# The second product of an MLP as seven half-block products a step

## The chip, the cores and the metric

The kernel runs on one core of one Trainium2 chip. The metric is the device time of one execution in microseconds (us), here the median of three runs. Engines are named as in the profile: PE is TensorE, DVE is VectorE, ACT is ScalarE, POOL is GpSimd, SP is SyncE, which here only starts transfers. SBUF is the memory that all engines work in; PSUM holds the eight banks of 128 x 512 float32 into which PE writes.

## The reference, cut to what matters

One encoder layer over 1024 tokens of width 1024 in float32: a layer norm, an input projection, two kinds of attention, their merge, an output projection with a layer norm, and an MLP with a layer norm. The change is in the MLP alone:

```
h = layer_norm(DEEPNORM_ALPHA * h + merged @ w_out[l], ln1_g[l], ln1_b[l])
u = jnp.square(jax.nn.relu(h @ w_ff1[l]))             # (1024, 4096)
h = layer_norm(DEEPNORM_ALPHA * h + u @ w_ff2[l], ln2_g[l], ln2_b[l])
```

## The kernel before, in words

**Matmuls in three parts.** Every float32 operand of a matmul is kept as a high part (a copy rounded to PE's format) and a low part (value less high part). `three` (L500) multiplies high by high, high by low and low by high into one bank: three matmuls of 128 x 128 by 128 x 512 for each product of tiles. ACT makes high parts by a copy, POOL low parts by a subtraction.

**The MLP in 16 steps.** A step takes 256 of the 4096 hidden channels, as two tiles n = 0, 1. On PE, `hidden(s, n, half)` (L722) makes one tile of the hidden layer for one half (512) of the tokens: 8 x 3 matmuls into one of the two GEMM banks. Four such pieces are a step's first product. `result(s, slot)` (L731) makes the second product of a step: 16 banks (8 tiles of tokens by 2 halves of the output's columns), each 2 x 3 matmuls, over a ring of four banks. `pe_step` (L753) runs the hidden pieces of step s and then the results of the step before, so u and w_ff2 have two slots each and the splits of a step lie beside 43 us of PE's work.

**DVE.** `square` (L1477) takes a piece from its bank with relu and squares it in place in SBUF. `dve_step` (L1488) does four squares and then adds the 16 banks of the step before to `res`, the running sums (L1498; L1496 in the first step, with the residual's factor).

**ACT and POOL.** `act_step` (L1024) and `pool_step` (L1143) split, a step: two tiles of w_ff1 (128 x 1024 each; L1030, L1148), two tiles of w_ff2 at once (128 x 2048; L1034, L1151) and four pieces of u (128 x 512; L1038, L1155).

**SP.** `load_step` (L466) asks for one tile of w_ff1 when the last one's low part is done (two transfers of 256 KB), and for w_ff2's two rows of tiles (1 MB).

**The order** is written out by hand: each engine runs its own list, in loops over pairs of steps, and the lists meet in semaphores: `gemm_done`, `freed_dve` (bank read by relu), `u_full_done`, `u_hi`, `u_lo`, `w2_loaded`, `w2_hi`, `w2_lo`, `w_hi_done`, `w_lo_done`, `ring_done` (a bank of results is finished), `ring_read` (DVE has added it). In a loop the number waited for is computed from the step's number.

**The end.** After the last step DVE adds the last 16 banks with their row sums (L1515), ACT centres and squares (`centre_last`, L820), POOL multiplies with the gain (`gain`, L1064), DVE norms (`norm`, L1227) and SP stores, tile by tile.

## Time and profile before

| | |
|---|---|
| median of 3 runs | 1890.22 us (1889.5 to 1893.3) |
| the profiled execution's own time | 1891.27 us |
| span of its profile | 1889.5 us |
| PE busy | 1827.4 us, 97% of the span |
| DVE, ACT, POOL busy | 879.2, 615.2, 592.6 us |
| mean granted clock of PE | 0.992 of full speed |

The page of a profile gives the busy time of each engine over the span, then the same in 40 slices, then groups of instructions by line of the kernel. A table by stretches gives it for any part. In the order of time each row is an instruction, or some merged, with its start, its duration and in brackets how long the engine stood before it and who ended that. Matmuls overlap, so their pace is read from their starts, not from their durations (0.39 us).

### The profile page before, as it was taken

Reading aid. Unit: us, or ns where it says so; the run is one execution under the profiler, and the core shown is the slowest. Engines: PE = TensorE matmul, PEld = TensorE weight load, DVE = VectorE, ACT = ScalarE, POOL = GpSimd, SP = SyncE. Lnnn points to the kernel's source line nnn. Section 1 sums busy time; section 2 is a strip of 40 time slices with the busy share of each in tenths; the row PEclk is TensorE's granted clock in tenths of the full one; section 3 lists DMA queues with packets and bytes.
Section 4 is the critical chain, followed back from the end, with each engine's and each line's share of the span. In section 5 each row is a group of like instructions: output and inputs, shape, how many; then the busy total and the mean of one; then the engine's idle time right before and its main releaser. Section 6 shows DMA issues by size and latency. Waiting matters only on the chain.

```text
span 1889.5 us, 24837 instructions
## 1 busy us (share of the span) xinstructions
PE 1827.4 (97%) x9175; PEld 1489.9 (79%) x9175; DVE 879.2 (47%) x2053; ACT 615.2 (33%) x1339; POOL 592.6 (31%) x562
## 2 busy tenths in 40 slices
PE   6999999999999999999999899999999999999996
PEld 4777777777778888888888678888888888888884
DVE  6366666665665552013423466333333333333337
ACT  5355554555556664201222301211111111111104
POOL 4312111121134443222222480633333333333324
PEclk9999999999999999999999999999999999999998
DMA  7311111111111111144222510311111111111102
GB/s 249 116 36 45 33 47 34 34 46 33 42 40 32 36 30 34 45 134 144 79 79 90 194 40 23 123 45 45 44 44 44 44 44 54 63 49 55 33 0 89
DMA packets 143142, 117.91 MB, mean 62 GB/s; under 512 B 23300, under 2 KB 129996, under 8 KB 143052
## 3 DMA queue, kind: packets, MB, share of 16 engines
q1 hardware_dynamic: 133836, 112.52, 18.9%
q10 hardware_dynamic: 9216, 4.20, 0.8%
q8 instruction: 55, 0.90, 0.2%
q14 instruction: 35, 0.29, 0.1%
HBM read 99.88 MB, written 21.53 MB: 64 GB/s over the span
## 4 chain that ended last, share of the span: by engine, by line
PE 84%; DVE 7%; issue 3%; ACT 3%; POOL 2%; DMA 0%; POOLq 0%; SPq 0%; DVEq 0%; ACTq 0%
PE bank L502 25%; PE bank L504 24%; PE bank L503 24%; PE bank L538 4%; PE bank L526 3%; PE bank L586 2%; DVE mix L1321 2%; ACT mix L886 1%; PE bank L587 1%; DVE mix L1300 1%; DVE res L1236 1%; DVE o_buf L1288 1%; POOL hT_lo L1081 1%; DVE y_hi L1184 0%; POOL y_lo L1137 0%
## 5 line engine op out<-in xcount | busy, mean ns | idle before, releaser
L502 PE MATMUL bank<-hT_hi,w_hi 128*128 128x512 f32 x1312 | 528.8, 403 | 9.1 <-POOL hT_lo L1081 5.4
L503 PE MATMUL bank<-hT_lo,w_hi 128*128 128x512 f32 x1312 | 513.4, 391 | 0.0
L504 PE MATMUL bank<-hT_hi,w_lo 128*128 128x512 f32 x1312 | 513.3, 391 | 0.0
L1060 POOL TENSOR_TENSOR w_lo<-w_raw,w_hi 128x256 fp32r<-128x256 f32 x264 | 196.4, 775 | 630.6 <-ACT w_hi L777 630.6
L502 PEld LDWEIGHTS bank<-hT_hi,w_hi 128*128 128x128 f32 x1312 | 247.3, 188 | 82.5 <-issue 14.1
L504 PEld LDWEIGHTS bank<-hT_hi,w_lo 128*128 128x128 f32 x1312 | 247.4, 189 | 53.9
L503 PEld LDWEIGHTS bank<-hT_lo,w_hi 128*128 128x128 f32 x1312 | 247.8, 189 | 46.5
L502 PE MATMUL bank<-y_hi 128*128 128x512 f32 (+1 forms) x604 | 228.6, 379 | 2.7 <-DVE small L1515 2.7
L503 PE MATMUL bank<-y_lo,y_hi 128*128 128x512 f32 (+1 forms) x604 | 225.8, 374 | 0.0
L504 PE MATMUL bank<-y_hi,y_lo 128*128 128x512 f32 (+1 forms) x604 | 225.5, 373 | 0.0
L1498 DVE TENSOR_TENSOR res<-res,bank 128x512 f32<-128x512 f32 x224 | 154.1, 688 | 141.2 <-PE bank L504 141.2
L1484 DVE TENSOR_SCALAR mix<-bank 128x512 f32<-128x512 f32 x64 | 44.3, 691 | 255.9 <-PE bank L504 255.9
L1151 POOL TENSOR_TENSOR y_lo<-mix,y_hi 128x2048 fp32r<-128x2048 f32 x16 | 73.7, 4606 | 254.4 <-ACT y_hi L1034 254.4
L1155 POOL TENSOR_TENSOR y_lo<-mix,y_hi 128x512 fp32r<-128x512 f32 x64 | 83.6, 1308 | 166.3 <-ACT y_hi L1038 166.3
L1038 ACT ACTIVATE y_hi<-mix 128x512 fp32r<-128x512 f32 x64 | 40.4, 632 | 283.6 <-DVE mix L1486 283.6
L502 PEld LDWEIGHTS bank<-y_hi 128*128 128x128 f32 x604 | 113.8, 188 | 23.9 <-DVE small L1515 3.8
L504 PEld LDWEIGHTS bank<-y_hi,y_lo 128*128 128x128 f32 x604 | 113.9, 189 | 20.2
L503 PEld LDWEIGHTS bank<-y_lo,y_hi 128*128 128x128 f32 x604 | 114.0, 189 | 20.0
L1321 DVE CUSTOM_DVE_ANT_0 mix<-bank,aux 128x512 f32<-128x512 f32 (+2 forms) x192 | 99.0, 553 | 64.9 <-PE bank L538 64.5
L1034 ACT ACTIVATE y_hi<-mix 128x2048 fp32r<-128x2048 f32 x16 | 30.7, 1917 | 266.7 <-PE bank L504 263.1
L886 ACT ACTIVATE mix<-mix,small 128x256 f32<-128x256 f32 (+7 forms) x128 | 98.3, 770 | 42.8 <-DVE small L1329 42.3
L504 PE MATMUL bank<-y_hi,w_lo 128*128 128x512 f32 x256 | 99.6, 389 | 0.0
(154 smaller groups left out, 2674.5 us busy)
## 6 DMA issues: line engine op xcount, KB each, us to landing
w_raw<-in_w_in_dram SPq DMA_DIRECT2D x100, 256.0 KB, 3.3
w_raw<-in_w_ff_dram SPq DMA_DIRECT2D x64, 256.0 KB, 3.0
mix<-in_w_ff_dram SPq DMA_DIRECT2D x16, 1024.0 KB, 7.1
bias_rows<-bias_line SPq DMA_DIRECT2D x3, 1536.0 KB
res<-in_x_dram SPq DMA_DIRECT2D x8, 512.0 KB, 7.1
x_spill<-res SPq DMA_DIRECT2D x8, 512.0 KB, 5.9
o_spill<-o_buf ACTq DMA_DIRECT2D x64, 64.0 KB, 1.6
w_raw<-in_w_branch_b_dram SPq DMA_DIRECT2D x16, 256.0 KB, 3.9
```

The source lines that it names most:

```text
L502: pe.matmul(bank, lhs[0], rhs[0], start=start, stop=False)
L503: pe.matmul(bank, lhs[0], rhs[1], start=False, stop=False)
L504: return pe.matmul(bank, lhs[1], rhs[0], start=False, stop=stop)
L526: mm = pe.transpose(TR[n % 2][:, at * P:(at + 1) * P], src, ident[:, :])
L538: mm = pe.matmul(SC[units[m] % 3][:, at:at + keys.stop - keys.start], queries[left][rows], k[right][rows, k_slot, keys], start=not (left o ...
L886: e = act.activation(s_a[:, i % 2, m, 0:(i + 1) * P], s_a[:, i % 2, m, 0:(i + 1) * P], ACT.Exp, bias=neg_max[:, i % 2, m:m + 1], accum_out ...
L1060: ins = pool.tensor_tensor(w[1][:, n % 2, at:at + 2], w_raw[:, at:at + 2, :], w[0][:, n % 2, at:at + 2].bitcast(F32), ALU.subtract)
L1151: pool.tensor_tensor(w2[1][:, slot], w2_raw, w2[0][:, slot].bitcast(F32), ALU.subtract).then_inc(w2_lo, 1)
L1155: pool.tensor_tensor(u[1][:, slot, n, cols], u_full[:, n, cols], u[0][:, slot, n, cols].bitcast(F32), ALU.subtract).then_inc(u_lo, 1)
L1321: dve.tensor_tensor_reduce(out=s_a[:, slot, m, lo:hi], in0=SC[n % 3][:, 0:hi - lo], in1=bias_a[:, h % 2, off + lo:off + hi], scale=1.0, sc ...
L1484: dve.tensor_scalar(u_full[:, n, cols], GEMM[half][:, :], 0.0, None, ALU.max).then_inc(freed_dve, 1)
L1498: ins = dve.tensor_tensor(res[:, t, cols], res[:, t, cols], RING[g % 4][:, :], ALU.add)
```

## The change

In steps 0 to 14 the second product is computed by Strassen's scheme in its form with seven products and shared sums. The matrices of a step are cut in two each way: u (256 hidden channels by 1024 tokens) into four blocks of 128 x 512, w_ff2's two rows of tiles into four blocks of 128 x 512. DVE forms four differences of w_ff2's blocks and four sums or differences of u's blocks (`form`); with three raw blocks of each side (one of them replaced in place) that makes seven left and seven right factors. Each of the seven products is 4 banks (128 tokens each) of 3 matmuls, 28 banks a step, over a ring of six banks: the two banks that transposes used join the ring. Each product has its own running sum over all 15 steps (`sums_of`: four in `res`, two in `mix`, one in the last rows of y's two halves), and the sums are folded into the output once, beside the last step's hidden pieces. The residual is prepared for this in step 0 (two subtractions on `res`). The last step is computed as before, with tokens 512 to 1023 first.

u and w_ff2 now have seven slots of 128 x 512, and one set of them: full values lie where their low parts will be, and the splits are done in place. `result(s)` follows the hidden pieces of the same step s, so there is no lag of a step any more; the loops run over single steps. The hidden pieces come in the order (0,0), (0,1), (1,1), (1,0) of tile and half of tokens. w_ff2 comes in two transfers of 512 KB a step, the upper row once two products of the step before are done, the lower once all are. ACT and POOL split 14 blocks of 128 x 512 a step and two tiles of w_ff1.

The diff, cut to its core. Lines that are only deleted stand in the functions above.

```diff
+FF_ORDER = [(0, 0), (0, 1), (1, 1), (1, 0)]
+U_SLOT = [0, 2, 3, 5]
+PRODUCTS, QUARTER = 7, 4
+PER_STEP = PRODUCTS * QUARTER
+RING0 = 2 * NT
+TAIL0 = RING0 + PER_STEP * (FF_STEPS - 1)
+TAIL = [4, 5, 6, 7, 0, 1, 2, 3]
+TAIL_W2 = [0, 1, 5, 6]
...
-        u = [t[:, 0:4, :].rearrange("p (s n) q -> p s n q", n=2) for t in y]
-        w2 = [t[:, 4:8, :].rearrange("p (s n) c -> p s n c", n=2) for t in y]
-        w2_raw = mix[:, 0:2, :]
-        u_full = mix[:, 2:4, :]
+        y_full = [nc.alloc_sbuf_tensor_at(f"y_full{i}", [P, KT, SEQ], F32, offset=y_at + i * KT * SEQ * 4) for i in range(2)]
+        (u, w2), (u_full, w2_full) = (
+            [[t[:, :, :].rearrange("p s k -> p (s k)")[:, at:at + PRODUCTS * HALF].rearrange("p (s q) -> p s q", s=PRODUCTS) for t in pair]
+             for at in (0, PRODUCTS * HALF)] for pair in (y, y_full))
+        u_full, w2_full = u_full[1], w2_full[1]
+        first_sum = [t[:, 7, :].rearrange("p (t c) -> p t c", t=2) for t in y_full]
+        sums_of = [[first_sum[t // 2][:, t % 2, :] for t in range(QUARTER)],
+                   [mix[:, 2 + t // 2, t % 2 * HALF:(t % 2 + 1) * HALF] for t in range(QUARTER)],
+                   [res[:, 4 + t, HALF:DM] for t in range(QUARTER)],
+                   [res[:, 4 + t, 0:HALF] for t in range(QUARTER)],
+                   [mix[:, t // 2, t % 2 * HALF:(t % 2 + 1) * HALF] for t in range(QUARTER)],
+                   [res[:, t, 0:HALF] for t in range(QUARTER)],
+                   [res[:, t, HALF:DM] for t in range(QUARTER)]]
...
+        RING6 = RING + [banks[5], banks[6]]
...
+            def load_w2(s, row):
+                if row == 0:
+                    sp.wait_ge(ring_done, s * PER_STEP + (RING0 - PER_STEP + 2 * QUARTER) if not isinstance(s, int) or s else RING0)
+                else:
+                    sp.wait_ge(ring_done, s * PER_STEP + RING0)
+                at = s * 2 + row
+                src = ff2[:, bass.ds(at if isinstance(s, int) else sp.snap(at), 1), :]
+                sp.dma_start(w2_full[:, 5 * row:5 * row + 2, :], src.rearrange("p n (h c) -> p (n h) c", h=2)).then_inc(w2_loaded[row], 16)
+            def load_ff1(s, n):
+                sp.wait_ge(w_lo_done, s * 2 + (FF0 + n))
+                col = s * (2 * P) + n * P
+                col = col if isinstance(s, int) else sp.snap(col)
+                for g in range(2):
+                    sp.dma_start(w_raw[:, g * 4:g * 4 + 4, :], ff1[:, g * 4:g * 4 + 4, bass.ds(col, P)]).then_inc(raw_loaded, 16)
+            load_ff1(0, 1)
+            load_w2(0, 0)
+            load_w2(0, 1)
+            load_ff1(0, 2)
             sp.wait_ge(h_rows, NT)
+            sp.wait_ge(ln_done, 2 * NT)
             sp.dma_start(ln_late[0], row(ln2_g)).then_inc(late_loaded, 16)
             sp.dma_start(ln_late[1], row(ln2_b)).then_inc(late_loaded, 16)
             with sp.Fori(1, FF_STEPS - 1) as s:
+                load_w2(s, 0)
+                load_ff1(s, 1)
+                load_w2(s, 1)
+                load_ff1(s, 2)
...
+            def hidden(s, k):
+                n, half = FF_ORDER[k]
                 pe.wait_ge(w_lo_done, s * 2 + (FF0 + n + 1))
+                pe.wait_ge(freed_dve, s * 4 + (MLP_FREED + k - 1))
                 for t in range(KT):
+                    mm = three(GEMM[k % 2][:, :], [a[:, n, t, :] for a in w],
                                [a[:, t, half * HALF:(half + 1) * HALF] for a in hT], t == 0, t == KT - 1)
                 mm.then_inc(gemm_done, 1)
+            def result(s):
+                for i in range(PRODUCTS):
+                    pe.wait_ge(w2_lo, s * PRODUCTS + (i + 1))
+                    pe.wait_ge(u_lo, s * PRODUCTS + (i + 1))
+                    for t in range(QUARTER):
+                        j = i * QUARTER + t
+                        pe.wait_ge(ring_read, s * PER_STEP + (RING0 + max(j - 5, 0)))
+                        three(RING6[j % 6][:, :], [a[:, i, t * P:(t + 1) * P] for a in u],
+                              [a[:, i, :] for a in w2], True, True).then_inc(ring_done, 1)
+            def last_result():
+                s = FF_STEPS - 1
+                pe.wait_ge(w2_lo, s * PRODUCTS + 4)
                 for g in range(2 * NT):
+                    t, half = TAIL[g // 2], g % 2
+                    if g % NT == 0:
+                        pe.wait_ge(u_lo, s * PRODUCTS + 3 + g // NT)
+                    pe.wait_ge(ring_read, TAIL0 + max(g - 3, 0))
+                    left = [U_SLOT[k] for k in ((0, 3) if t < 4 else (1, 2))]
                     for n in range(2):
+                        mm = three(RING[g % 4][:, :], [a[:, left[n], t % 4 * P:(t % 4 + 1) * P] for a in u],
+                                   [a[:, 5 * n + half, :] for a in w2], n == 0, n == 1)
                     mm.then_inc(ring_done, 1)
+            for piece in range(4):
+                n, half = FF_ORDER[piece]
+                if piece == 1:
+                    pe.wait_ge(ln_done, 2 * NT)
+                    for b in range(2):
+                        transposes(("h1", NT - 1, b))
+                if n == 0:
+                    pe.wait_ge(tr_lo, BATCH[("h1", 4 * half + 3, 1)] + 1)
+                hidden(0, piece)
+            result(0)
+            with pe.Fori(1, FF_STEPS - 1) as s:
+                for piece in range(4):
+                    hidden(s, piece)
+                result(s)
+            for piece in range(4):
+                hidden(FF_STEPS - 1, piece)
+            last_result()
...
+            ff1_hi(0, 1)
+            with act.Fori(0, FF_STEPS - 1) as s:
+                act.wait_ge(w2_formed, s * 4 + 1)
+                w2_high(0)
+                act.wait_ge(w2_formed, s * 4 + 4)
+                for slot in range(1, PRODUCTS):
+                    w2_high(slot)
+                act.wait_ge(u_formed, s * 4 + 1)
+                for slot in (0, 1):
+                    u_high(slot)
+                act.wait_ge(u_formed, s * 4 + 3)
+                for slot in (2, 3, 4):
+                    u_high(slot)
+                ff1_hi(s, 2)
+                act.wait_ge(u_formed, s * 4 + 4)
+                for slot in (5, 6):
+                    u_high(slot)
+                ff1_hi(s, 3)
...
+            ff1_lo(0, 1)
+            with pool.Fori(0, FF_STEPS - 1) as s:
+                for slot in range(PRODUCTS):
+                    w2_low(s, slot, slot)
+                u_low(s, 0, 0)
+                pool.wait_ge(u_formed, s * 4 + 3)
+                for slot in (1, 2, 3):
+                    u_low(s, slot, slot)
+                ff1_lo(s, 2)
+                pool.wait_ge(u_formed, s * 4 + 4)
+                for slot in (4, 5, 6):
+                    u_low(s, slot, slot)
+                ff1_lo(s, 3)
...
+            def square(s, k):
                 dve.wait_ge(gemm_done, s * 4 + (2 * FF0 + k + 1))
+                block = u_full[:, U_SLOT[k], :]
+                dve.tensor_scalar(block, GEMM[k % 2][:, :], 0.0, None, ALU.max).then_inc(freed_dve, 1)
                 dve.wait_ge(freed_dve, s * 4 + (MLP_FREED + k + 1))
+                dve.tensor_tensor(block, block, block, ALU.mult).then_inc(u_full_done, 1)
+            def form(blocks, dst, a, op, b, signal):
+                dve.tensor_tensor(blocks[:, dst, :], blocks[:, a, :], blocks[:, b, :], op).then_inc(signal, 1)
             def dve_step(s):
+                dve.wait_ge(w2_loaded[0], s * 16 + 16)
+                form(w2_full, 2, 1, ALU.subtract, 0, w2_formed)
+                square(s, 0)
+                dve.wait_ge(w2_loaded[1], s * 16 + 16)
+                dve.wait_ge(w2_formed, s * 4 + 1)
+                form(w2_full, 4, 6, ALU.subtract, 2, w2_formed)
+                dve.wait_ge(w2_formed, s * 4 + 2)
+                form(w2_full, 3, 5, ALU.subtract, 4, w2_formed)
+                form(w2_full, 1, 6, ALU.subtract, 1, w2_formed)
+                square(s, 1)
+                dve.wait_ge(u_full_done, s * 4 + 2)
+                form(u_full, 1, 0, ALU.subtract, 2, u_formed)
+                if isinstance(s, int):
+                    for t in range(0, QUARTER, 2):
+                        dve.tensor_tensor(res[:, t:t + 2, HALF:DM], res[:, t:t + 2, HALF:DM], res[:, 4 + t:6 + t, HALF:DM], ALU.subtract)
+                square(s, 2)
+                dve.wait_ge(u_formed, s * 4 + 1)
+                dve.wait_ge(u_full_done, s * 4 + 3)
+                form(u_full, 4, 3, ALU.subtract, 1, u_formed)
+                form(u_full, 2, 2, ALU.add, 3, u_formed)
+                square(s, 3)
+                dve.wait_ge(u_full_done, s * 4 + 4)
+                form(u_full, 6, 5, ALU.subtract, 4, u_formed)
+                for j in range(PER_STEP):
+                    i, total = j // QUARTER, sums_of[j // QUARTER][j % QUARTER]
+                    dve.wait_ge(ring_done, s * PER_STEP + (RING0 + j + 1))
+                    bank = RING6[j % 6][:, :]
+                    if not isinstance(s, int):
+                        ins = dve.tensor_tensor(total, total, bank, ALU.add)
+                    elif i in (0, 1, 4):
+                        ins = dve.tensor_copy(total, bank)
                     else:
+                        ins = dve.scalar_tensor_tensor(total, total, ALPHA, bank, ALU.mult, ALU.add)
                     ins.then_inc(ring_read, 1)
+            dve_step(0)
+            with dve.Fori(1, FF_STEPS - 1) as s:
+                dve_step(s)
+            def fold(a, b):
+                return dve.tensor_tensor(a, a, b, ALU.add)
+            p6, p7 = ([mix[:, at + n, :].rearrange("p (t c) -> p t c", t=2) for n in range(2)] for at in (0, 2))
+            right, low_left, low_right = ([res[:, at + 2 * n:at + 2 * n + 2, cols] for n in range(2)]
+                                          for at, cols in ((0, slice(HALF, DM)), (4, slice(0, HALF)), (4, slice(HALF, DM))))
+            dve.wait_ge(ring_read, TAIL0)
             for n in range(2):
+                ins = fold(p6[n], first_sum[n])
+            link(ins)
+            square(FF_STEPS - 1, 0)
+            for n in range(2):
+                fold(p7[n], p6[n])
+            for n in range(2):
+                ins = fold(right[n], low_right[n])
+            link(ins)
+            square(FF_STEPS - 1, 1)
+            for n in range(2):
+                fold(low_left[n], p7[n])
+            square(FF_STEPS - 1, 2)
+            for n in range(2):
+                fold(low_right[n], p7[n])
+            for n in range(2):
+                ins = fold(right[n], p6[n])
+            link(ins)
+            square(FF_STEPS - 1, 3)
+            dve.wait_ge(folded, 2)
...
```

## Rows read from the trace of the kernel before

**Rows 1.** The page, part 1: busy time of each engine over the span
```profile
PE 1827.4 (97%) x9175; PEld 1489.9 (79%) x9175; DVE 879.2 (47%) x2053; ACT 615.2 (33%) x1339; POOL 592.6 (31%) x562
```

**Rows 2.** Table by stretches: one MLP step, then the whole steady MLP
```profile
core 0: us, PE busy (x) PEld busy (x) DVE busy (x) ACT busy (x) POOL busy (x), PEclk, DMA share, GB/s
1216.00:1259.52 43.52, 43.52 (x194) 36.04 (x193) 16.75 (x24) 6.34 (x7) 14.49 (x7) 1.00 0.16 50
1216.00:1847.50 631.50, 631.50 (x2788) 522.90 (x2787) 246.21 (x354) 88.53 (x98) 201.82 (x98) 1.00 0.14 45
```

**Rows 3.** PE in order of time across a bank's end (start, duration)
```profile
1617.13 0.39 PE L504 MATMUL bank<-y_hi,y_lo 128*128 128x512 f32 x1
1617.35 0.39 PE L502 MATMUL bank<-y_hi 128*128 128x512 f32 x1
1617.58 0.39 PE L503 MATMUL bank<-y_lo,y_hi 128*128 128x512 f32 x1
```

**Rows 4.** Groups by line, 1216 to 1847 us (xcount, busy us, mean ns)
```profile
L1498 DVE TENSOR_TENSOR res<-res,bank 128x512 f32<-128x512 f32 x223 | 153.4, 688 | 140.5 <-PE bank L504 140.5
...
L1155 POOL TENSOR_TENSOR y_lo<-mix,y_hi 128x512 fp32r<-128x512 f32 x57 | 73.8, 1294 | 160.8 <-ACT y_hi L1038 160.8
L1148 POOL TENSOR_TENSOR w_lo<-w_raw,w_hi 128x1024 fp32r<-128x1024 f32 x27 | 64.8, 2398 | 0.0
...
L1484 DVE TENSOR_SCALAR mix<-bank 128x512 f32<-128x512 f32 x57 | 39.4, 692 | 235.7 <-PE bank L504 235.7
```

**Rows 5.** DVE in order of time, two places where it waits for nothing
```profile
1608.76 0.69 DVE L1486 TENSOR_TENSOR mix<-mix 128x512 f32<-128x512 f32 x1
1609.39 0.69 DVE L1498 TENSOR_TENSOR res<-res,bank 128x512 f32<-128x512 f32 x1
...
1872.65 0.68 DVE L1515 CUSTOM_DVE_ANT_0 res<-res,bank 128x512 f32<-128x512 f32 x1
...
1873.26 0.68 DVE L1515 CUSTOM_DVE_ANT_0 res<-res,bank 128x512 f32<-128x512 f32 x1
```

**Rows 6.** DVE and POOL in order of time, an add beside a split
```profile
1611.45 2.41 POOL L1148 TENSOR_TENSOR w_lo<-w_raw,w_hi 128x1024 fp32r<-128x1024 f32 x1
...
1612.12 0.69 DVE L1498 TENSOR_TENSOR res<-res,bank 128x512 f32<-128x512 f32 x1 [0.67 <-PE bank L504]
```

**Rows 7.** DVE and POOL in order of time, squares beside splits
```profile
1178.04 2.41 POOL L1148 TENSOR_TENSOR w_lo<-w_raw,w_hi 128x1024 fp32r<-128x1024 f32 x1 [48.63 <-ACT w_hi L1030]
...
1178.48 2.51 DVE L1486 TENSOR_TENSOR mix<-mix 128x512 f32<-128x512 f32 x1
...
1185.85 2.99 POOL L1155 TENSOR_TENSOR y_lo<-mix,y_hi 128x512 fp32r<-128x512 f32 x2
```

**Rows 8.** The page, part 6: DMA issues (KB each, us to landing)
```profile
w_raw<-in_w_ff_dram SPq DMA_DIRECT2D x64, 256.0 KB, 3.0
...
mix<-in_w_out_dram SPq DMA_DIRECT2D x8, 512.0 KB, 4.9
```

**Rows 9.** PE in order of time around the MLP's first hidden piece
```profile
1168.93 1.04 PE L526 MATMUL bank<-ident,res 128*128 128x128 f32 x8
1169.72 0.47 PE L502 MATMUL bank<-hT_hi,w_hi 128*128 128x512 f32 x1
...
1177.90 0.50 PE L502 MATMUL bank<-hT_hi,w_hi 128*128 128x512 f32 x1 [1.57 <-DVE hT_lo L1184]
```

**Rows 10.** The last step: DVE, then PE, in order of time
```profile
1856.78 3.40 DVE L1236 SCALAR_TENSOR_TENSOR res<-res,small,bias_b_buf 128x1024 f32<-128x1024 f32 x1
...
1869.57 0.72 PE L502 MATMUL bank<-y_hi 128*128 128x512 f32 x1 [1.85 <-DVE small L1515]
1870.09 0.63 PE L503 MATMUL bank<-y_lo,y_hi 128*128 128x512 f32 x1
```

**Rows 11.** ACT in order of time
```profile
1609.49 0.63 ACT L1038 ACTIVATE y_hi<-mix 128x512 fp32r<-128x512 f32 x1 [4.72 <-DVE mix L1486]
1610.02 1.05 ACT L1030 ACTIVATE w_hi<-w_raw 128x1024 fp32r<-128x1024 f32 x1
```

167 lines of the change are left out of this document (49 added, 118 removed).

## The prediction, made before the changed kernel was run

> **What bounds the kernel now.** The page first: TensorE (PE) is busy 97% of the span, VectorE (DVE) 47%, GpSimd (POOL) 31% [rows 1]. Busy shares can't say whether PE ever waits, so next the table by stretches over the MLP: in one step of 43.52 us PE is busy for all of it, DVE for 16.75, POOL for 14.49, ACT for 6.34, and over 631.5 us the picture is the same at a granted clock of 1.00, the 2.4 GHz level [rows 2]. Last the order of time on PE: one matmul of 512 columns starts each 0.2267 us (0.22 and 0.23 in turn), and the start of the next bank, with its wait on `ring_read` and its signal, costs nothing [rows 3]. A step is 192 such matmuls, 192 x 0.2267 = 43.5 us. So from 1178 us to 1847 us nothing but the number of matmuls sets the time. A measurement of this kernel can tell about 0.2% (3.8 us) from no change.
>
> **What goes.** The second product of a step is 16 banks of 6 matmuls (96). With the seven products it is 28 banks of 3 (84). 12 fewer in each of 15 steps: 180 x 0.2267 = **-40.8 us**, all on the path. That is the best the change can do, as the last step and the first products keep their counts.
>
> **More banks, more signals.** A bank is now finished each 3 x 0.2267 = 0.68 us, not each 1.36 us. [Rows 3] show no gap at a bank's end, so I take 0 for the signals and hold the first part of the waits' cost for a rival below. The Trainium skill (TensorE: Matmul & The Clock Gate, "The cost: per-tile semaphore tail") gives 26.3 ns for each increment of a matmul, one after the other; 12 more in each of 15 steps would give back 4.7 us, an estimate from that page. The trace does not show such a cost at the bank's end.
>
> **DVE, the ring.** It must add 28 banks a step, in the 19.04 us in which PE makes them. One add is 0.688 us [rows 4], longer than 0.68. But an operation that waits for nothing starts before the one ahead has ended: an add 0.63 us after a square, one PSUM read 0.61 us after another [rows 5]. So the pace is 0.61 to 0.69, and I take 0.61: DVE just keeps up, and what it is late at the start it wins back only at 0.07 us a bank. Adds are not hurt by POOL: one of the usual 0.69 us lies inside a POOL operation of 2.41 us [rows 6].
>
> **DVE, the start of the ring.** Before, the results lagged a step behind, so DVE had nothing to prepare. Now, after the last hidden piece ends (call it E), DVE has relu, square and one block difference ahead of its first add: 0.69 + 0.72 + 0.69 = 2.1 us (relu in [rows 4], square in [rows 5], a difference taken like it; the square starts 0.03 after relu has ended). The first add ends at E + 2.8. PE has six banks and needs the first of them back at E + 6 x 0.68 = E + 4.1. Alone that is 1.3 us to spare. It isn't alone. An operation of DVE with both inputs in SBUF and one of POOL exclude each other: the square issued at 1178.48 ran 2.51 us, until 0.54 us after POOL's operation ended; the POOL pair of 1185.85 took 2.99 instead of 2 x 1.29, as a square of DVE's came in between [rows 7]. At E POOL is working off the halves of u and then the 2.4 us split of w_ff1, nearly without a pause. Square and difference can each wait for a whole operation of 1.29 us (ending 0.55 us behind it, so 1.15 later than alone). The first add then ends between E + 2.8 and E + 5.1, and PE stands 0 to 1.0 us a step; with the 2.4 us split in between, up to 2.1. I take a little over the middle of the first, 0.55, as POOL hardly pauses there: 15 x 0.55 = **+8 us**. Once it has stood, PE is again ahead only as far as the ring, but DVE is then the faster, so the step pays once. After a stand of 1.57 us the next matmul took 0.50 us [rows 9]; after one of 1.85 us two took 0.72 and 0.63, the half level of the clock, 1.2 GHz [rows 10]. I count nothing for the clock with stands of about 1 us, 41 us apart.
>
> **POOL and ACT.** POOL gets 14 splits of 128x512 and 2 of 128x1024: 14 x 1.294 + 2 x 2.40 = 22.9 us in place of 14.5 [rows 4]; with 12 DVE operations (4 squares, 8 differences) that may each hold it 0.55 us it is 29.5 of 40.8 us. ACT: 14 x 0.63 + 2 x 1.05 = 10.9 us [rows 11]. Both fit, but their order must too. Counted from a step's start: first piece ends at 5.4, square and three differences of w_ff2 by 9, six splits on POOL (7.8 plus three DVE operations in between) by 18.5, the first half of u by 20.4. PE wants it at 21.76. The cover is 1.4 us, so 0, but the thinnest of all. Product 1 (at 24.5) needs u_lo two at about 22, and the later ones have 3 us and more.
>
> **SP and the loads.** w_ff2 now comes as two loads of 512 KB; such a load took 4.9 us and one of 256 KB 3.0 [rows 8]. The lower row is asked for when the last bank is done and is wanted by DVE 7 us later, behind the first square; cover 2 us. The w_ff1 tile is queued behind a wait for eight banks, until 27 us into the step; load, ACT and POOL bring it to 35, and it is wanted at 51. The upper row has more. Nothing for these; if the 7 us of hidden work were gone the lower row would cost its 4.9.
>
> **Step 0.** There the pipeline of before had step 1's hidden products over the splits. Now result(0) follows at once. DVE is free at 1177.9, with the stand for the last transposes [rows 9]. Its first square meets POOL's 2.41 us split as before, the three differences end near 1184, and POOL's six splits (7.8) with five DVE operations in between, two of them 1024 wide and 1.1 us each (about 4), end near 1196.5, the first half of u near 1198. PE is ready at 1177.9 + 3 pieces of 5.44 = 1194.3. That is **+4 us**, 0 to 6.
>
> **The end.** The last step keeps 16 banks of six. Before, DVE had 0.67 us to spare on each bank [rows 6] until the first norm, an operation of 3.40 us behind POOL, from which on it was itself the bound [rows 10]. Now it comes some 1.1 us late to the first bank (last fold, relu, square) and catches up 0.75 us a bank while banks are 1.36 us apart: **+0.5 us**, 0 to 2.5.
>
> **Sum**: -40.8 + 8 + 4 + 0.5 = -28 us. The profiled execution took 1891.27 us by the clock of the runs (span 1889.5 us), 1 us above the median of 1890.22. 1891.3 - 28.3 gives 1863.0; against the median 1862. I forecast **1862 us**, with 1855 (stand of 0.25 us a step, 2 us in step 0) to 1872 (1.0 us a step, 6 and 2 at the ends) as this case's own range. Chance 0.58.
>
> **Rival 1, nothing stands.** If POOL happens to be between operations at E in the settled rhythm (the phases repeat each step, so it is the same each time), the 1.3 us to spare holds and the steps are 40.8 us. -40.8 + 0.5 + 0 to 4: 1850 to 1854. For it: 29.5 of 40.8 us on POOL leave pauses. Against: the order puts its fullest stretch there. Chance 0.20.
>
> **Rival 2, a thin cover tears.** The 1.4 us ahead of product 0 is used up, or the 2.4 us split sits ahead of the difference: 1.5 to 2.1 us a step, 22 to 32 us, with 4.5 to 6.5 at the ends: 1876 to 1888. Chance 0.12.
>
> **Rival 3, DVE becomes the bound (slower).** Place: DVE's whole cycle. 4 relus at 0.72, 12 operations with two SBUF inputs, each waiting for a whole POOL operation (1.85 us), and 28 adds at 0.69 rather than 0.61: 2.9 + 22.2 + 19.3 = 44.4 us. It decides from a cycle over 43.5 us. 15 x 0.9 + 4 + 0.5 = +18: 1908 us. Against: POOL has only 16 operations a step, and eight of the twelve have hidden time in front of them. The Trainium skill (SBUF — State Buffer, "Who interferes with whom") says that the loser "fully blocks"; by that rule such waits are whole operations. The trace agrees, with the 2.51 us of [rows 7]. Chance 0.05.
>
> **Rival 4, PE's sequencer (slower).** The seven products hold 42 waits on computed values in 19 us, where there were 18 in 22. Eight transposes with their loads start in 0.79 us [rows 9], so an instruction takes PE at most 0.05 us to issue; 168 are 8.3 us. A wait may then cost (19.04 - 8.3) / 42 = 0.26 us before it shows and 0.32 before all is lost. Bounds: [rows 3] alone allow 0.76; ACT issued an operation with two such waits 0.53 us behind another [rows 11], so 0.24 at most on ACT, nearest in kind. At 0.35 the products take 23.0 us and a step is 1.24 us longer than before: +23 with the ends, 1913 us. Chance 0.03.
>
> **Rival 5, it does not do what it says**: matmuls fall but the time stays, as every saved one becomes a wait: 1887 to 1893. Nothing in the rows speaks for it. Chance 0.02.
>
> **Numbers.** The range of 8 in 10 takes my case and rival 1 nearly whole (0.78) and reaches toward rival 2: 1851 to 1875. Faster by over 0.2%: 0.58 + 0.20 + 0.12 = 0.90; within: 0.02 (rival 5); slower: 0.05 + 0.03 = 0.08 (rivals 3 and 4).
>
> **What the profile after would show.** PE: 84 matmuls of the second product a step, each 0.2267 us apart; a step's length 40.8 (rival 1), 41.1 to 41.8 (mine), 42.3 or more (rival 2), with the stand at the seventh bank of the products and released by DVE's first add. If it stands ahead of product 0 and is released by POOL, the cover on w_ff2 tore. DVE: squares and differences of 0.7 to 1.9 us, adds at 0.61 us for most of the ring. A first add that ends later than E + 5.1, adds more than 0.68 us apart all through, or a PE row at the half level of the clock would make me wrong. PE spacing above 0.2267 with no releaser named would be rival 4. The first result would start near 1198.

## The result, and the profile after

| | before | after |
|---|---|---|
| median | 1891.37 us (4 runs, 1889.5 to 1893.3) | 1877.47 us (4 runs, 1874.85 to 1880.41) |
| the profiled execution | 1891.27 us, span 1889.5 | 1880.41 us, span 1878.6 |
| mean granted clock of PE | 0.992 | 0.987 |

The ratio is 0.9923, interval 0.9911 to 0.9936: faster by 13.9 us, half of the 28 us forecast. The time lies 2.5 us above the range.

"After" is the changed kernel. A stand, here and below, is time in which PE waits. It is given either as the row's bracket or from start to start; the second is about 0.4 us longer, as it takes in the matmul before.

The page of after, engine line. DVE has gone from 47% to 61% and POOL from 31% to 40%, and PE, with 180 matmuls less, from 97% to 96%.

```profile
PE 1799.9 (96%) x8995; PEld 1462.3 (78%) x8995; DVE 1141.4 (61%) x2367; ACT 668.1 (36%) x1477; POOL 757.7 (40%) x702
```

The table by stretches of after, columns as in [rows 2]: step 0's last three hidden pieces with the stand behind them; step 0's products; a settled step; its products alone; all 14 settled steps; the last step's hidden pieces; its results and the end.

```profile
1181.06:1201.24 20.18, 16.62 (x73) 13.47 (x73) 19.87 (x17) 6.17 (x13) 17.42 (x10) 0.98 0.26 79
1201.24:1223.12 21.88, 21.88 (x84) 17.92 (x85) 20.23 (x29) 3.63 (x5) 13.01 (x8) 0.87 0.15 48
1514.86:1556.53 41.67, 41.10 (x182) 33.73 (x180) 32.34 (x45) 9.86 (x16) 24.66 (x16) 1.00 0.16 50
1536.62:1556.53 19.91, 19.34 (x86) 15.70 (x84) 19.64 (x30) 4.15 (x6) 12.58 (x8) 1.00 0.17 53
1223.12:1806.48 583.36, 575.44 (x2521) 472.18 (x2520) 452.52 (x617) 139.14 (x226) 345.31 (x224) 1.00 0.17 50
1806.48:1834.20 27.72, 24.80 (x97) 19.98 (x96) 26.32 (x18) 3.05 (x5) 19.45 (x9) 0.88 0.05 19
1834.20:1878.60 44.40, 24.44 (x97) 18.75 (x95) 36.09 (x69) 21.19 (x33) 21.77 (x9) 0.82 0.24 95
```

Read the first column against what PE needs. The 72 hidden matmuls are 16.3 us at full pace, and took 20.18. The 84 of the products are 19.04; they took 21.88 in step 0 and 19.91 in a settled step. The 96 hidden ones are 21.76 and took 27.72 in the last step. The granted clock is 0.87 and 0.88 in step 0's products and in the last hidden pieces: there PE ran part of the time at its lower level. The 0.82 of the last row is not new: over the same stretch of the kernel before, 42.31 us, it is 0.81. A settled step is 583.36 / 14 = 41.67 us, 1.85 less than the 43.52 of [rows 2], where the matmuls alone would give 2.72.

The order of time on PE in that settled step, at the seventh bank. [Rows 3] are the bank's end before: nothing in brackets. Now PE waits once a step, for DVE's first add.

```profile
1540.47 0.39 PE L544 MATMUL bank<-y_hi,y_lo 128*128 128x512 f32 x1
1541.43 0.50 PE L542 MATMUL bank<-y_hi 128*128 128x512 f32 x1 [0.57 <-DVE y_full L1596]
1541.77 0.39 PE L543 MATMUL bank<-y_lo,y_hi 128*128 128x512 f32 x1
```

From start to start that is 0.96 us in place of 0.2267, and the next one comes 0.34 behind: 0.73 + 0.11, nearly all of the 0.87 us that the products take too long. DVE at the same place (relu, square, last block difference, adds), and POOL beside it:

```profile
1536.82 0.69 DVE L1560 TENSOR_SCALAR y_full<-bank 128x512 f32<-128x512 f32 x1 [0.93 <-PE bank L544]
1537.55 1.53 DVE L1562 TENSOR_TENSOR y_full<-y_full 128x512 f32<-128x512 f32 x1
1539.12 1.67 DVE L1565 TENSOR_TENSOR y_full<-y_full 128x512 f32<-128x512 f32 x1
1540.71 2.47 DVE L1596 TENSOR_TENSOR y_full<-y_full,bank 128x512 f32<-128x512 f32 x4
1543.10 2.47 DVE L1596 TENSOR_TENSOR mix<-mix,bank 128x512 f32<-128x512 f32 x4
```
```profile
1535.97 4.26 POOL L1219 TENSOR_TENSOR y_lo<-y_full,y_hi 128x512 fp32r<-128x512 f32 x3 [1.23 <-DVE y_full L1565]
1540.20 2.84 POOL L1211 TENSOR_TENSOR w_lo<-w_raw,w_hi 128x1024 fp32r<-128x1024 f32 x1
```

Relu has its usual 0.69 us; the square and the difference, 0.7 alone, take 1.53 and 1.67, as POOL works without a pause from 1535.97. The adds, one operand in a bank, run 0.60 us apart (1540.71 to 1543.10, four of them).

### The profile page after: what moved, and what is told of

Same layout as the page of the kernel before. It is cut to its first block, busy times and chain, and to the rows that moved or that the text cites. A ratio compares the mean times of both kernels' runs of the same rounds, so it can differ in the third digit from the quotient of the medians.

```text
span 1878.6 us, 25778 instructions
## 1 busy us (share of the span) xinstructions
PE 1799.9 (96%) x8995; PEld 1462.3 (78%) x8995; DVE 1141.4 (61%) x2367; ACT 668.1 (36%) x1477; POOL 757.7 (40%) x702
## 4 chain that ended last, share of the span: by engine, by line
PE 74%; DVE 10%; issue 7%; POOL 5%; ACT 3%; DVEq 0%; DMA 0%; POOLq 0%; ACTq 0%
PE bank L542 22%; PE bank L543 21%; PE bank L544 21%; PE bank L578 4%; PE bank L566 3%; PE bank L626 2%; DVE mix L1400 2%; DVE y_full L1562 1%; POOL res L1191 1%; POOL res L1195 1%; ACT mix L937 1%; PE bank L627 1%; DVE res L1609 1%; DVE y_full L1560 1%; DVE mix L1379 1%
## 5 line engine op out<-in xcount | busy, mean ns | idle before, releaser
L1215 POOL TENSOR_TENSOR y_lo<-y_full,y_hi 128x512 fp32r<-128x512 f32 x109 | 158.4, 1482 | 187.2 <-ACT y_hi L1082 181.7
L542 PE MATMUL bank<-y_hi 128*128 128x512 f32 (+1 forms) x544 | 208.3, 383 | 16.1 <-DVE y_full L1596 7.9
L543 PE MATMUL bank<-y_lo,y_hi 128*128 128x512 f32 (+1 forms) x544 | 203.9, 375 | 0.0
L544 PE MATMUL bank<-y_hi,y_lo 128*128 128x512 f32 (+1 forms) x544 | 203.7, 374 | 0.0
L1219 POOL TENSOR_TENSOR y_lo<-y_full,y_hi 128x512 fp32r<-128x512 f32 x109 | 154.0, 1437 | 29.2 <-DVE y_full L1565 17.2
L1082 ACT ACTIVATE y_hi<-y_full 128x512 fp32r<-128x512 f32 x109 | 60.3, 621 | 228.6 <-DVE y_full L1565 218.8
L1596 DVE TENSOR_TENSOR res<-res,bank 128x512 f32<-128x512 f32 x224 | 136.2, 681 | 0.0
L1565 DVE TENSOR_TENSOR y_full<-y_full 128x512 f32<-128x512 f32 x120 | 126.0, 1070 | 2.1
L1085 ACT ACTIVATE y_hi<-y_full 128x512 fp32r<-128x512 f32 x109 | 62.2, 623 | 172.6 <-DVE y_full L1565 147.8
L1560 DVE TENSOR_SCALAR y_full<-bank 128x512 f32<-128x512 f32 x64 | 44.2, 691 | 128.3 <-PE bank L544 128.2
L1211 POOL TENSOR_TENSOR w_lo<-w_raw,w_hi 128x1024 fp32r<-128x1024 f32 x31 | 80.9, 2611 | 96.9 <-ACT w_hi L1079 96.9
L544 PEld LDWEIGHTS bank<-y_hi,y_lo 128*128 128x128 f32 x544 | 103.3, 190 | 18.1
```

The lines of the kernel that those rows point to most:

```text
L542: pe.matmul(bank, lhs[0], rhs[0], start=start, stop=False)
L543: pe.matmul(bank, lhs[0], rhs[1], start=False, stop=False)
L544: return pe.matmul(bank, lhs[1], rhs[0], start=False, stop=stop)
L1211: pool.tensor_tensor(w[1][:, n % 2], w_raw[:, :, :], w[0][:, n % 2].bitcast(F32), ALU.subtract).then_inc(w_lo_done, 1)
L1215: pool.tensor_tensor(w2[1][:, slot, :], w2_full[:, slot, :], w2[0][:, slot, :].bitcast(F32), ALU.subtract).then_inc(w2_lo, 1)
L1219: pool.tensor_tensor(u[1][:, slot, :], u_full[:, slot, :], u[0][:, slot, :].bitcast(F32), ALU.subtract).then_inc(u_lo, 1)
```

## Account of the time

Profiled spans, after against before. Ahead of the MLP the code is the same, but the first hidden piece begins at 1172.91 against 1169.72 [rows 9]: 3.2 us that no edit explains (the twelve profiles of this study lie between 1167.98 and 1173.42). Inside the MLP, each stretch beside the time PE needs for its matmuls or the time that the same stretch took in the kernel before:

| stretch | after | needed or before | us |
|---|---|---|---|
| 180 matmuls less | | | -40.8 |
| step 0, three pieces and stand | 20.18 | 16.49 | +3.7 |
| step 0, products | 21.88 | 19.04 | +2.8 |
| 14 settled products | 19.91 | 19.04 | +12.2 |
| last hidden pieces | 27.72 | 21.76 | +6.0 |
| last results to the end | 44.40 | 42.31 | +2.1 |

The sum is -14.0; with the 3.2 of the start it is the 10.9 us between the two profiled spans. That -14.0 is also the difference of the medians is partly chance: the profiled execution was the longest of its four and carries step 0's slow matmuls, which not every execution has (experiment 8). So three things are to be tested: the stand of a settled step, the slow matmuls of step 0, and the 8.1 us at the end.

Step 0's products and the last hidden pieces, in the order of time on PE. In both places a stand is followed by matmuls that last 0.63 us and start 0.43 us apart, twice the usual 0.22 to 0.23.

```profile
1197.29 0.39 PE L544 MATMUL bank<-hT_hi,w_lo 128*128 128x512 f32 x1
1201.24 0.77 PE L542 MATMUL bank<-y_hi 128*128 128x512 f32 x1 [3.56 <-issue]
1201.80 0.63 PE L543 MATMUL bank<-y_lo,y_hi 128*128 128x512 f32 x1
...
1825.88 0.77 PE L542 MATMUL bank<-hT_hi,w_hi 128*128 128x512 f32 x1 [2.92 <-DVE y_full L1560]
1826.45 0.63 PE L543 MATMUL bank<-hT_lo,w_hi 128*128 128x512 f32 x1
```

DVE in the same last hidden pieces: the folds of the seven sums (L1609, two of 128x1024 in each row) around relu and square. At 1825.05 it reads a bank for which PE has been waiting.

```profile
1812.19 0.69 DVE L1560 TENSOR_SCALAR y_full<-bank 128x512 f32<-128x512 f32 x1 [1.22 <-PE bank L544]
1812.92 2.10 DVE L1562 TENSOR_TENSOR y_full<-y_full 128x512 f32<-128x512 f32 x1
1814.94 5.64 DVE L1609 TENSOR_TENSOR mix<-mix 128x1024 f32<-128x1024 f32 x2
1820.50 4.51 DVE L1609 TENSOR_TENSOR res<-res 128x1024 f32<-128x1024 f32 x2
1825.05 0.69 DVE L1560 TENSOR_SCALAR y_full<-bank 128x512 f32<-128x512 f32 x1
```

## Experiments

### 1. Unused matmuls for the two stands

```diff
+            for n in range(15):
+                pe.matmul(banks[6][:, :], hT[0][:, 0, 0:P], hT[0][:, 0, 0:HALF], start=True, stop=True)
             result(0)
...
             for piece in range(4):
+                if piece == 2:
+                    pe.wait_ge(ring_read, TAIL0)
+                    for n in range(12):
+                        pe.matmul(banks[6][:, :], hT[0][:, 0, 0:P], hT[0][:, 0, 0:HALF], start=True, stop=True)
                 hidden(FF_STEPS - 1, piece)
```

> Nothing is left out. 15 matmuls whose result is not used are put ahead of the first seven products, and 12 ahead of the third hidden piece of the last step, where PE stood 3.56 and 2.92 us and then ran 14 matmuls at the half level of the clock each time. Theory (the stands let the clock fall, and the slow matmuls behind them are half of what each stand costs): PE has no long stand at the two places, the products of step 0 take 19.0 to 19.3 us instead of 21.88, the last hidden pieces 24.7 to 25.1 instead of 27.72, all others stay, and the whole is 5 to 6 us faster than the changed kernel, 1872. Rival (the clock costs nothing on the path, as DVE and POOL are the bound behind each stand): the two stretches stay within 0.5 us of what they were, since the waits only move, and the time stays at 1877.

Measured: 1876.7 us (1875.7 to 1877.83), ratio 0.9914 [0.9898, 0.9931]. Step 0's products took 19.12 us, 2.8 less, as PE came to them without a stand:

```profile
1201.40 0.47 PE L542 MATMUL bank<-y_hi 128*128 128x512 f32 x1 [0.19 <-issue]
1201.71 0.39 PE L543 MATMUL bank<-y_lo,y_hi 128*128 128x512 f32 x1
```

At the end the filling was put ahead of the third hidden piece, but the stand is ahead of the fourth, 72 matmuls behind 1806.48, where PE waits for the relu of the second piece (1825.05 in after). The filling took up the time all the same, and PE ran at full clock up to the last results. Nothing was won, as the rival had it: the last hidden pieces took 27.03 us with the filling, a stand of 2.32 us (from start to start) appeared ahead of the last results, and the end took 45.03; 72.1 together, and 27.72 + 44.40 = 72.1 in after. There DVE is late whether PE's matmuls are slow or not. That it was the filling that kept the clock up in step 0 this one profile doesn't show: in experiments 3 and 8 the clock stayed up there without it. The whole differs from after by less than the runs scatter.

### 2. Without step 0's two subtractions

It leaves out the preparation of the residual.

```diff
-                if isinstance(s, int):
-                    for t in range(0, QUARTER, 2):
-                        dve.tensor_tensor(res[:, t:t + 2, HALF:DM], res[:, t:t + 2, HALF:DM], res[:, 4 + t:6 + t, HALF:DM], ALU.subtract)
```

> Left out: the two subtractions of 1024 wide blocks on the residual in step 0 (L1582). Theory (they hold DVE for 4.55 us and POOL's w_ff2 splits with it, and so make most of the 3.56 us stand ahead of product 0): the stand falls to 0 to 1.5 us, the clock does not fall, and from the last transposes to the second step's hidden pieces it is 5 to 6.5 us less. Rival (the stand is POOL's own queue of eight splits): the stand loses only the 2 us in which the two operations held POOL, stays at 1.5 us or more, and the clock decides the rest.

Measured: 1871.9 us (one run). The stand ahead of step 0's products was 1.61 us where it was 3.56, so just above the theory's 1.5 and what the rival said: the two operations made 1.9 us of it, POOL's own queue the rest (experiment 6). The pieces and the stand took 18.24 us, 1.9 less. The products took 19.16, with no slow matmul, but the clock can stay up there without this edit too (experiment 8). The two operations that the prediction did count (1.1 us each) cost 4.55 us together in the profile of after, beside POOL's splits, and 1.9 of them came through to PE. The rest of the time won here is the start at 1169.11 rather than 1172.91.

The end has the change's own code in this run, and the last hidden pieces ran at full clock:

```profile
1797.99:1825.00 27.01, 22.21 (x98) 17.79 (x96) 25.57 (x18) 3.05 (x5) 19.44 (x9) 1.00 0.07 20
```

From here to the end it is 1870.1 - 1797.99 = 72.1 us, as in after, where the clock was 0.88 in this stretch. So slow matmuls in the last hidden pieces cost nothing that can be seen.

### 3. Without the folds

It leaves out the twelve folds of DVE and the two of POOL.

```diff
-            for n in range(2):
-                ins = fold(p6[n], first_sum[n])
-            link(ins)
...
             square(FF_STEPS - 1, 0)
-            for n in range(2):
-                fold(p7[n], p6[n])
-            for n in range(2):
-                ins = fold(right[n], low_right[n])
-            link(ins)
             square(FF_STEPS - 1, 1)
...
-            dve.wait_ge(folded, 2)
```

> Left out: the twelve folds of running sums on DVE (L1609) and the two on POOL (L1239) in the last step. Theory (the folds make DVE late with relu and squares, and so the whole loss behind step 14): the last hidden pieces take 21.8 us instead of 27.72, and from the last products' first matmul to the end it is 42 to 43 us as in the kernel before (44.4 in the changed one); 7.5 to 8.5 us in all. Rival (the loss is the missing lag, since the last products follow their own hidden pieces at once): the hidden pieces shorten by less than 3 us or the end stays at 44.4.

Measured: 1868.39 us (one run), span 1866.6. The table by stretches, for the same four parts as in after (step 0's pieces, its products, last hidden pieces, the end):

```profile
1179.70:1199.86 20.16, 16.60 (x72) 13.44 (x73) 19.85 (x17) 6.14 (x13) 17.43 (x10) 1.00 0.28 79
1199.86:1219.00 19.14, 19.14 (x84) 15.85 (x85) 19.11 (x29) 3.64 (x5) 13.09 (x8) 1.00 0.19 56
1802.53:1824.29 21.76, 21.76 (x98) 18.02 (x96) 5.60 (x8) 3.05 (x5) 8.96 (x7) 1.00 0.09 25
1824.29:1866.60 42.31, 22.71 (x97) 17.60 (x95) 33.37 (x66) 21.41 (x33) 21.64 (x9) 0.84 0.24 99
```

The last two rows are 21.76 and 42.31: exactly the kernel before. So all of the 8.1 us at the end is the folds' doing. DVE is busy 5.60 us in the last hidden pieces where it was 26.32, so the twelve folds, with what the squares lost beside them, took 20.7 us there. The first two rows show something else. The stand is the same 3.56 us, but behind it the clock does not fall:

```profile
1199.86 0.47 PE L542 MATMUL bank<-y_hi 128*128 128x512 f32 x1 [3.56 <-issue]
1200.17 0.39 PE L543 MATMUL bank<-y_lo,y_hi 128*128 128x512 f32 x1
```

### 4. The square reads the bank

PE's next piece then waits for the square, not for relu (in step 0 from the third piece on). POOL has no part in an operation of DVE that reads a bank, if the theory is right.

```diff
-                pe.wait_ge(freed_dve, s * 4 + (MLP_FREED + k - 1))
+                if isinstance(s, int) and s == 0 and k < 2:
+                    pe.wait_ge(freed_dve, MLP_FREED + k - 1)
+                else:
+                    pe.wait_ge(u_full_done, s * 4 + (k - 1))
...
-                dve.tensor_tensor(block, block, block, ALU.mult).then_inc(u_full_done, 1)
+                dve.tensor_tensor(block, block, GEMM[k % 2][:, :], ALU.mult).then_inc(u_full_done, 1)
```

> Nothing is left out. The square multiplies relu's value in SBUF with the value still in the bank (the product is the same), so it has one input in SBUF only; the bank is free 0.7 us later. Theory (the 0.87 us that each settled step loses is the wait of square and difference for POOL): the square after the fourth piece takes 0.69 instead of 1.53 us, the first add ends 0.3 to 0.9 us earlier, the products' stretch is 19.0 to 19.4 us instead of 19.91, the time 5 to 12 us less with the ends. Rival (the stand is set by how fast DVE adds, or by POOL's order, in which the difference then waits longer): the stretch stays at 19.7 us or more.

Measured: 1858.77 us (1858.3 to 1860.01), ratio 0.9822 [0.9806, 0.9838]. The groups by line over the settled steps, squares only, after (L1562) and this kernel (L1565, 55 of the 56 in the window asked for); columns: count | busy us, mean ns | idle before it:

```profile
L1562 DVE TENSOR_TENSOR y_full<-y_full 128x512 f32<-128x512 f32 x56 | 66.2, 1183 | 1.9
```
```profile
L1565 DVE TENSOR_TENSOR y_full<-y_full,bank 128x512 f32<-128x512 f32 x55 | 37.8, 688 | 1.9
```

A settled step here, first in the table by stretches, then on DVE:

```profile
1500.00:1540.80 40.80, 40.80 (x182) 33.78 (x181) 30.01 (x45) 9.86 (x16) 23.33 (x16) 1.00 0.17 51
...
1564.01 0.69 DVE L1563 TENSOR_SCALAR y_full<-bank 128x512 f32<-128x512 f32 x1 [1.83 <-PE bank L544]
1564.74 0.69 DVE L1565 TENSOR_TENSOR y_full<-y_full,bank 128x512 f32<-128x512 f32 x1
1565.46 1.16 DVE L1568 TENSOR_TENSOR y_full<-y_full 128x512 f32<-128x512 f32 x1
1566.55 2.47 DVE L1599 TENSOR_TENSOR y_full<-y_full,bank 128x512 f32<-128x512 f32 x4
```

The square takes 0.69 us each time and the first add starts 2.54 us behind relu's start, not 3.89. All 14 settled products took 19.04 us: no stand at all, and no cost of 28 signals. One operand moved is worth 14 x 0.87 = 12.2 us there. Between the profiled spans (1878.6 and 1857.2) the rest is 4.4 us in step 0 (18.58 + 19.13, no slow matmuls), 2.2 in the last hidden pieces (25.52), 3.1 from an earlier start of the MLP (1169.78), less 0.4 at the end (44.8); between the medians it is 18.7 us in all (16.6 against the median of experiment 8). Of step 0's 4.4 us, 2.8 are the slow matmuls, which come and go without an edit.

### 5. The folds spread evenly

On top of 4: four, two, three and three folds ahead of the four squares of the last step, where they were two, four, two and four.

```diff
+            for n in range(2):
+                ins = fold(p7[n], p6[n])
+            link(ins)
             square(FF_STEPS - 1, 0)
-            for n in range(2):
-                fold(p7[n], p6[n])
...
+            fold(low_right[0], p7[0])
             square(FF_STEPS - 1, 2)
-            for n in range(2):
-                fold(low_right[n], p7[n])
+            fold(low_right[1], p7[1])
```

> The kernel of e4_square_bank with the twelve folds of the last step in another order on DVE: four ahead of the first square, then two, three and three, where it was two, four, two and four. Nothing is left out. Theory (the fold in front of a relu is what PE waits for): the last hidden pieces take 21.8 to 24.0 us instead of 25.5, the products of that step start without a long stand, the tail from them to the end stays at 44 to 45 us, and the time is 1.5 to 3.5 us less, 1856. Rival (DVE's whole work in these 21.8 us is too much, with 14.4 us of folds, 5.6 of squares and the waits for POOL): the stand only moves behind, to the first of the last products, and the time stays within 1 us of 1858.8.

Measured: 1863.53 us (1860.12 to 1863.97), ratio 0.9839 [0.9822, 0.9855]. The theory fell. The last hidden pieces and the stand behind them took 26.05 us, more than in 4 (25.52), and the stand only moved, from the fourth piece to the first of the last results (0.66 us of it to the third piece):

```profile
1818.18 0.47 PE L542 MATMUL bank<-y_hi 128*128 128x512 f32 x1 [3.23 <-issue]
1818.48 0.53 PE L543 MATMUL bank<-y_lo,y_hi 128*128 128x512 f32 x1
```

From the first of these pieces to the end of the kernel it was 70.1 us, and 70.4 in 4: with this other order nothing is won, which speaks for too much work on DVE there rather than a wrong order of it. Step 0 has the same code as in 4 and a stand of the same length (2.33 against 2.36 us from start to start), but this time slow matmuls behind it (20.76 against 19.13 us). That and a start of the MLP at 1173.42 rather than 1169.78 are the whole 5.0 us by which this profile is longer than that of 4; neither comes from the edit.

### 6. POOL's order in front of product 0

On top of 5: the split of u's first half comes after four of w_ff2's seven blocks, not after all.

```diff
-                for slot in range(PRODUCTS):
+                for slot in range(4):
                     w2_low(s, slot, slot)
                 u_low(s, 0, 0)
+                for slot in range(4, PRODUCTS):
+                    w2_low(s, slot, slot)
```

> The kernel of e5_folds_spread, and POOL does the first half of u behind four of the seven w_ff2 blocks instead of behind all seven, in all fifteen steps. Nothing is left out. Theory (in step 0 product 0 waits for POOL's queue, and the settled steps have room): the 18.6 us of step 0's last three hidden pieces and the stand become 16.5 to 17.2, a stand of at most 1 us moves behind product 0, settled products stay at 19.04, the time falls by 1 to 2 us. Rival (the queue as a whole is late, so what product 0 gains product 1 or 2 loses): the sum of the stretch and of step 0's products (37.7 us) stays the same.

Measured: 1858.52 us (1857.28 to 1859.64), ratio 0.9816 [0.98, 0.9832]. The stand ahead of step 0's products is gone. A short one has come up at the second product, 12 matmuls on, and no slow matmul follows it:

```profile
1196.82 0.39 PE L542 MATMUL bank<-y_hi 128*128 128x512 f32 x1
...
1200.23 0.47 PE L542 MATMUL bank<-y_hi 128*128 128x512 f32 x1 [0.53 <-issue]
```

Pieces and products of step 0 took 16.47 + 19.85 = 36.3 us, 3.0 less than in 5 (18.59 + 20.76) and 1.4 less than in 4, which had no slow matmuls either: of the 2.1 us taken from the stand 0.7 come back at the second product. What made PE stand in step 0 was POOL's queue. In after the low part of u's first half, last in that queue, ends at 1201.14, and PE starts the first product at 1201.24:

```profile
1199.43 1.71 POOL L1219 TENSOR_TENSOR y_lo<-y_full,y_hi 128x512 fp32r<-128x512 f32 x1
```

### 7. A ring of four

After, with four banks in the ring in place of six.

```diff
-        RING6 = RING + [banks[5], banks[6]]
+        RING6 = RING
...
-                        pe.wait_ge(ring_read, s * PER_STEP + (RING0 + max(j - 5, 0)))
-                        three(RING6[j % 6][:, :], [a[:, i, t * P:(t + 1) * P] for a in u],
+                        pe.wait_ge(ring_read, s * PER_STEP + (RING0 + max(j - 3, 0)))
+                        three(RING6[j % 4][:, :], [a[:, i, t * P:(t + 1) * P] for a in u],
```

> The changed kernel with the ring of results at four banks, as before the change, instead of six. Nothing is left out. Theory (the settled stand is the first add's lateness against the ring's depth): PE stands at the fifth bank, 2.72 us after the last hidden piece, until the first add ends, 4.6 us after it; a products' stretch is 21.2 to 21.5 us instead of 19.91, and the kernel is about 20 us slower than the changed one, near 1897 and slower than the one before. Rival (the stand comes from somewhere else, such as the pace of adds or of the splits): the stretch stays within 0.5 us of 19.91.

Measured: 1911.9 us (one run; before 1892.9 on the same chip), clock 0.979: with this ring the change would be slower than the kernel before. Two banks fewer take 1.36 us of cover away, and each settled step stands about 1.35 us longer (2.27 to 2.32 us from start to start). That was the theory, and it gave 1897 us. In three of the 14 steps the products took 21.2 us, as it said, but in eleven 22.83 to 22.91, with seven or eight matmuls 0.43 us apart; these 11 x 1.6 = 18 us were not in it. One of the three and one of the eleven (the wait is for the first add):

```profile
1244.79 0.50 PE L542 MATMUL bank<-y_hi 128*128 128x512 f32 x1 [1.88 <-DVE y_full L1596]
1245.13 0.40 PE L543 MATMUL bank<-y_lo,y_hi 128*128 128x512 f32 x1
...
1464.79 0.55 PE L542 MATMUL bank<-y_hi 128*128 128x512 f32 x1 [1.93 <-DVE y_full L1596]
1465.14 0.63 PE L543 MATMUL bank<-y_lo,y_hi 128*128 128x512 f32 x1
```

### 8. The change once more

No edit; it asks which of the small things in the account come back.

> The changed kernel unchanged, for the scatter of its runs. Theory (each of two stands of about 3 us, ahead of product 0 and in the last hidden pieces, lets the clock fall in some executions and not in others, 2.8 us each): runs spread over 3 to 6 us, and the mean granted clock is lower in the longer ones; settled steps stay at 41.67 us. Rival (the scatter is that of the part ahead of the MLP, as in the kernel before): clock and time don't go together.

Measured: 1875.34 us (1871.9 to 1877.13), ratio 0.9904 [0.9885, 0.9923]. Step 0's pieces and stand 20.18, settled products 19.87, from the last hidden pieces to the end 72.1 us: all again. Step 0's products took 19.17, not 21.88: the same stand, and here no slow matmuls.

```profile
1199.41 0.47 PE L542 MATMUL bank<-y_hi 128*128 128x512 f32 x1 [3.56 <-issue]
1199.72 0.39 PE L543 MATMUL bank<-y_lo,y_hi 128*128 128x512 f32 x1
```

Of the 5.0 us between the two profiled spans 2.7 are this, 1.9 the start of the MLP (1171.06 against 1172.91) and 0.5 the settled steps, so theory and rival each hold in part. Over its four runs the mean clock hardly orders the times: 0.990 at 1871.9 us, 0.991 at 1875.31, 0.989 at 1875.37 and at 1877.13.

### 9. Bank square and POOL's order, folds as in the change

```diff
-                dve.tensor_tensor(block, block, block, ALU.mult).then_inc(u_full_done, 1)
+                dve.tensor_tensor(block, block, GEMM[k % 2][:, :], ALU.mult).then_inc(u_full_done, 1)
...
-                for slot in range(PRODUCTS):
+                for slot in range(4):
                     w2_low(s, slot, slot)
                 u_low(s, 0, 0)
+                for slot in range(4, PRODUCTS):
+                    w2_low(s, slot, slot)
```

> The kernel of e4_square_bank with the order of POOL of e6_pool_order, and the folds in the changed kernel's own order. Nothing is left out. Theory (the two edits act at different places, and the spreading of folds only moved a stand): step 0's three pieces with the stand, and its products, are 36.3 us together as in e6_pool_order (37.7 in e4_square_bank), the last hidden pieces 25.5 as in e4_square_bank, the time 1856 to 1858, about 35 us less than the kernel before. Rival (the gain of e6_pool_order's first steps was chance of the clock): the time is that of e4_square_bank, 1858.8, within 0.5 us.

Measured: 1857.98 us (five runs, 1856.09 to 1860.62; before 1890.86), ratio 0.9823 [0.9806, 0.9839]. Step 0 took 16.47 + 19.86 us as in 6, but the whole can't be told from 4 or from 6. These three are the best versions: some 33 us faster than the kernel before, 17 to 19 faster than the change.

### 10. Without POOL's two folds

9, with the two folds left out that POOL does beside DVE's.

```diff
-            for n in range(2):
-                pool.tensor_tensor(res[:, 2 * n:2 * n + 2, 0:HALF], res[:, 2 * n:2 * n + 2, 0:HALF], first_sum[n], ALU.add).then_inc(folded, 1)
```

> Left out: POOL's two folds of a running sum in the last step (L1242 of e9_bank_and_order); DVE's twelve stay. Theory (in the last step DVE's folds and POOL's work take turns: 12 x 1.1 us on DVE, 2 x 2.4 and 8 x 1.29 on POOL, 28 us in all where the hidden pieces last 21.8): the last hidden pieces lose about 3 of their 3.7 us over 21.8. Rival (DVE's own folds are too many for their places, whatever POOL does): the pieces lose less than 1 us.

Measured: 1857.69 us (one run, the MLP starting 2.9 us later than in 9). The last hidden pieces in 9, then here, in the table by stretches:

```profile
1785.84:1811.10 25.26, 22.18 (x98) 17.79 (x96) 23.76 (x18) 3.06 (x5) 19.98 (x9) 1.00 0.07 21
```
```profile
1788.75:1810.88 22.13, 21.92 (x97) 17.86 (x96) 20.63 (x18) 3.06 (x5) 12.37 (x7) 1.00 0.08 25
```

3.1 us less, and just as much less from there to the end of the kernel (67.2 for 70.3, where the kernel before took 64.1). DVE's two folds on `res` in 9, then here:

```profile
1798.07 4.53 DVE L1614 TENSOR_TENSOR res<-res 128x1024 f32<-128x1024 f32 x2
```
```profile
1800.03 2.35 DVE L1612 TENSOR_TENSOR res<-res 128x1024 f32<-128x1024 f32 x2
```

The same two operations on the same tiles: 1.18 us each with POOL idle beside them, 2.27 with POOL at work.

## Why the prediction was wrong in size, point by point

**What goes, -40.8 us: right.** 84 matmuls of the second product a step, 0.2267 us apart. Experiment 4 shows the settled step at exactly 40.80 us.

**Signals and waits, 0: right.** 28 banks in 19.04 us leave nothing for them in experiment 4, and so nothing for rival 4. The Trainium skill (TensorE: Matmul & The Clock Gate, "The cost: per-tile semaphore tail") gives 26.3 ns for each increment. The 4.7 us that the prediction estimated from it did not appear in this trace.

**DVE's pace on the ring, 0.61 us: right.** It was 0.60, and PE stood once a step, at the seventh bank, released by the first add, as said.

**The settled stand, 15 x 0.55 = +8: right in kind, too small in size.** It was 0.87 in each settled step, inside the bounds of 0 to 1.0. The prediction said that POOL hardly pauses there and still took little over the middle; the phases repeat, and the seventh bank started 0.93 to 0.97 us behind the sixth's last matmul in every settled step. Over 14 steps it is 12.2 us, +4 against the sum. Experiment 4 shows the cause: with the square out of POOL's way the stand is gone. Experiment 7 shows that the first add against the ring's depth sets its length.

**Step 0, +4: right.** Pieces and stand took 3.7 us more; the first result, forecast near 1198, came at 1201.24, and at 1198.0 if the later start is taken off. Experiment 6 shows POOL's queue as the cause, experiment 2 that the two operations on the residual made 1.9 us of it.

**The clock, counted at 0: failed.** The text did name a PE row at the half level as what would make it wrong, with [rows 10] in hand, but weighed only the stands of 1 us, not the 4 us it had itself put ahead of step 0's products. In the profiled execution it cost 2.8 us there. It is a cost of some executions: experiments 3 and 8 have the same stand without it. At the end it cost nothing to be seen: from the last hidden pieces on it was 72.1 us at a clock of 0.88, 0.94 and 1.00 in these pieces (after, experiments 8 and 2).

**"The end", +0.5: failed, the largest miss.** It came to +8.1. The working priced what lies between the last piece and the first result (last fold, relu, square) and put nothing on the hidden pieces ahead of it, without a reason. It never added up DVE's list beside them: twelve folds of 128x1024 at 1.18 us alone (14.1) and eight short operations (5.6) are 19.7 of 21.76 us, so the list is full even before POOL takes its turns. With them it was 26.32 busy of 27.72. Experiment 3 gives the 8.1 us back to the last tenth, experiment 10 shows that in the improved kernel, where 6.2 of it were left, 3.1 come from two operations on POOL, and experiment 5 that one other order of the folds wins nothing.

**The four together.** The settled stand is +4 against the sum, step 0 nearly 0, the clock +3, the end +7.6: -28.3 became -14.0.

**POOL and ACT's order in the settled steps, 0: right**, and the same for the loads: no wait for either shows in a settled step. POOL's splits of 128x512 took 1.42 us on average against 1.29 [rows 4]; this stayed under cover.

**The rivals.** Rival 1 (nothing stands) did not happen in the change, and is what experiment 4 made of the settled steps. Rival 2's time, 1876 to 1888, is where the result fell, but by another way: no cover on w_ff2 tore and the settled stand was not 1.5 us. Rival 3 did not come: DVE was busy 32.34 of 41.67 us. The Trainium skill (SBUF — State Buffer, "Who interferes with whom") says that an instruction of DVE with two inputs in SBUF contends with one of GpSimd that reads SBUF, and that one with at most one such input, outside certain faster modes, does not. The settled steps agree: operations with both inputs in SBUF were lengthened (the square to 1.18 us on average), those with one in a bank were not (0.68 and 0.69).
